# Last layer: four context slots left out of the projection, delta-rule preparation at two slots a tile

## What is computed

```python
for layer in range(DEPTH):
    need_ctx = layer < DEPTH - 1
    ...
def mixer(hc, hl, cos, sin, w_in, ..., need_ctx):
    pl = split_proj(hl @ w_in)
    pc = split_proj(hc @ w_in)
    r_l, r_c = retention_group(pc[0:4], pl[0:4], cos, sin, ret_rate, ret_norm_w, need_ctx)
    s_l, s_c = swa_group(pc[4:7], pl[4:7], cos, sin, sinks, need_ctx)
    g_l, g_c = gdn_group(pc[7:13], pl[7:13], conv_w, a_log, dt_bias, gdn_norm_w, need_ctx)
```

## Time and profile before

| | us |
|---|---|
| median of three runs | 3745.65 |
| their range | 3743.29 to 3751.66 |
| span of the profiled execution | 3739.8 |
| median less span | 5.85 |
| TensorE busy (of the span) | 3358.0 (90%) |
| VectorE busy | 1620.2 (43%) |
| ScalarE busy | 1050.0 (28%) |
| GpSimd busy | 670.9 (18%) |

### The profile page before, as it was taken

The page is one execution under the profiler, slowest core; times in us unless marked ns, Lnnn a source line. Parts: engine busy times, 40 slices in busy tenths (PEclk is TensorE's granted clock), DMA queues, the critical chain, the costliest instruction groups (busy, mean ns, idle before and its releaser), DMA issues. The chain is left out here.

```text
span 3739.8 us, 56640 instructions
## 1 busy us (share of the span) xinstructions
PE 3358.0 (90%) x21880; PEld 2813.4 (75%) x21880; DVE 1620.2 (43%) x2715; ACT 1050.0 (28%) x1921; POOL 670.9 (18%) x762
## 2 busy tenths in 40 slices
PE   6989847987899999999998989857887999999998
PEld 3878735866778888888887878746775778888886
DVE  4465775632352322223236365765633343322234
ACT  3244134612222121121213244134512231122112
POOL 1142763222000000000001142762222000000000
PEclk8999967998899999999999999967997999999998
DMA  4465285086401111111112466185194111111111
GB/s 175 145 195 189 71 276 159 18 240 199 162 28 39 40 38 35 39 39 39 34 39 83 147 192 198 62 279 150 27 274 172 57 45 51 45 50 46 50 50 62
DMA packets 245475, 396.49 MB, mean 106 GB/s; under 512 B 75811, under 2 KB 147747, under 8 KB 244902
## 3 DMA queue, kind: packets, MB, share of 16 engines
q1 hardware_dynamic: 239462, 374.03, 32.0%
q0 software_dynamic: 5824, 19.93, 1.4%
HBM read 280.27 MB, written 101.52 MB: 102 GB/s over the span
## 5 line engine op out<-in xcount | busy, mean ns | idle before, releaser
L1021 PE MATMUL ffn_bank<-ffn_h_hi,ffn_w_hi 128*128 128x512 f32 (+1 forms) x1760 | 651.4, 370 | 8.0 <-DVE ffn_h_lo L409 7.7
L1024 PE MATMUL ffn_bank<-ffn_h_lo,ffn_w_hi 128*128 128x512 f32 (+1 forms) x1760 | 649.1, 369 | 0.0
L1025 PE MATMUL ffn_bank<-ffn_h_hi,ffn_w_lo 128*128 128x512 f32 (+1 forms) x1760 | 648.6, 369 | 0.0
L924 PE MATMUL frt_acc<-frt_w_hi,frt_h_hi 128*128 128x472 f32 x960 | 377.3, 393 | 48.5 <-DVE frt_w_lo L803 27.6
L1021 PEld LDWEIGHTS ffn_bank<-ffn_h_hi,ffn_w_hi 128*128 128x128 f32 x1760 | 333.1, 189 | 72.3 <-DVE ffn_h_lo L409 13.2
L1025 PEld LDWEIGHTS ffn_bank<-ffn_h_hi,ffn_w_lo 128*128 128x128 f32 x1760 | 333.0, 189 | 55.3
L1024 PEld LDWEIGHTS ffn_bank<-ffn_h_lo,ffn_w_hi 128*128 128x128 f32 x1760 | 333.2, 189 | 54.2
L924 PE MATMUL frt_acc<-frt_w_hi,frt_h_lo 128*128 128x472 f32 x960 | 368.0, 383 | 0.0
L924 PE MATMUL frt_acc<-frt_w_lo,frt_h_hi 128*128 128x472 f32 x960 | 367.5, 383 | 0.0
L1015 DVE TENSOR_TENSOR ffn_w_lo<-ffn_raw,ffn_w_hi 128x1024 fp32r<-128x1024 f32 x132 | 161.7, 1225 | 469.2 <-ACT ffn_w_hi L1007 463.9
L1021 PE MATMUL ffn_bank<-ffn_a_hi,ffn_w_hi 128*128 128x512 f32 (+1 forms) x880 | 324.3, 368 | 0.8 <-DVE ffn_a_lo L1103 0.8
(11 more groups left out here) (370 smaller groups left out, 5597.5 us busy)
## 6 DMA issues: line engine op xcount, KB each, us to landing
ffn_raw<-w_ffn SPq DMA_DIRECT2D x132, 512.0 KB, 3.5
x<-ada_w SPq DMA_DIRECT2D x15, 2048.0 KB, 9.3
proj<-frt_out SPq DMA_DIRECT2D x120, 236.0 KB, 2.0
x<-proj SPq DMA_DIRECT2D x60, 384.0 KB, 4.5
frt_raw<-w_in SPq DMA_DIRECT2D x96, 236.0 KB, 4.4
met_pr<-proj SPq DMA_DIRECT2D x20, 704.0 KB, 6.1
met_vn<-pack SPq DMA_DIRECT2D x20, 640.0 KB, 6.7
pack<-frt_side SPq DMA_DIRECT2D x40, 256.0 KB, 2.5
```

Source lines behind the costliest of these rows:

```text
L924: mm = pe.matmul(acc[q % NA][:, 0:GW], a[:, k, tok], b[:, k, :], start=(k == 0 and i == 0), stop=(k == KC - 1 and i == 2))
L1021: mm = pe.matmul(out, w_hi, b_hi, start=first, stop=False)
L1024: pe.matmul(out, w_hi, b_lo, start=False, stop=False)
L1025: return pe.matmul(out, w_lo, b_hi, start=False, stop=last)
```

## The change

Attention values, keys and queries change places: values at 1552, keys at 1680, queries at 1808 to 2319; the gates stay. In the last layer the slots of tiles 0 and 1 are left out of groups whose first column is at or past `S_Q`, which is groups 4 (1888) and 5 (2360). Slots 0 to 39 are as before, group 4 is slots 40 to 47, group 5 slots 48 to 55. `base(j)` becomes `15 + 2 * j` in the last layer, so `SOLVE` is 39 there; `LATE` becomes 14. In both layers `meet` loads 1536 columns (the values lie between retention values and keys now, unused there), and the two adds of lines 1529 and 1530 become one of 640 columns.

```diff
-S_Q, S_K, S_V = 1552, 2064, 2192
+S_V, S_K, S_Q = 1552, 1680, 1808
-COLUMNS = ((2816, 16), (1792, 768), (0, 768), (1024, 768), (768, 256), (2560, 256))
+COLUMNS = ((2816, 16), (1792, 768), (0, 768), (1664, 128), (1536, 128), (1024, 512), (768, 256), (2560, 256))
...
-        SLOTS = GROUPS * TILES
+        WORK = [(g, t) for g in range(GROUPS) for t in range(TILES) if layer + 1 < DEPTH or t * P >= CTX or g * GW < S_Q]
+        SLOTS = len(WORK)
+        first_of = [min(q for q in range(SLOTS) if WORK[q][0] == g) for g in range(GROUPS)]
...
+        STEP = 12 if layer + 1 < DEPTH else 10
...
-            return 15 + (12 * j) // 5
+            return 15 + (STEP * j) // 5
...
-                for q in range(SOLVE):
-                    g, t = divmod(q, TILES)
+                for q in range(max(SOLVE, first_of[GROUPS - 2])):
+                    g, t = WORK[q]
...
-                LATE = 12
+                LATE = 2 * (first_of[GROUPS - 1] - SOLVE) - 4
...
-                    sp.dma_start(pr[u][:], proj[row:row + P, R_Q:R_Q + 1408]).then_inc(ins[u], 16)
+                    sp.dma_start(pr[u][:], proj[row:row + P, R_Q:R_Q + 1536]).then_inc(ins[u], 16)
...
-                    dve.tensor_tensor(hot[:, 0:512], hot[:, 0:512], swp[u][:, 0:512], ALU.add)
-                    dve.tensor_tensor(hot[:, 1024:1152], hot[:, 1024:1152], swp[u][:, 1024:1152], ALU.add)
-                    side = lambda ap: ap[:, 512:1024].rearrange("p (u c n) -> p u c n", u=2, c=4)
+                    dve.tensor_tensor(hot[:, 0:640], hot[:, 0:640], swp[u][:, 0:640], ALU.add)
+                    side = lambda ap: ap[:, 640:1152].rearrange("p (u c n) -> p u c n", u=2, c=4)
```

More of the change, by code:

```diff
@@ L632, in _ @@
                 for q in range(SLOTS):
-                    g, t = divmod(q, TILES)
-                    if t == 1 and g + 1 < GROUPS:
+                    g, t = WORK[q]
+                    if q == first_of[g] + 1 and g + 1 < GROUPS:
                         weights(g + 1)
@@ L679, in split_hi @@
                         else:
-                            act.wait_ge(psum_done, g * TILES)
+                            act.wait_ge(psum_done, first_of[g])
                         act.activation(w_hi[:, k, :], raw[:, k, :], ACT.Copy).then_inc(w_rounded, 1)
@@ L918, in project @@
                     for k in range(KC):
-                        if t == 0:
+                        if q == first_of[g]:
                             pe.wait_ge(w_split, g * KC + k + 1)
@@ L1281, in meet @@
         b_y, b_g, b_u = [st.ps(f"b_{n}", [P, 512]) for n in "ygu"]
-        pr, rp = [[st.sb(f"{n}{u}", shape) for u in range(NR)] for n, shape in (("pr", [P, 1408]), ("rp", [P, 2, 64]))]
+        pr, rp = [[st.sb(f"{n}{u}", shape) for u in range(NR)] for n, shape in (("pr", [P, 1536]), ("rp", [P, 2, 64]))]
         hot, swp = st.sb("hot", [P, 1152]), dual("swp", [P, 1152])
@@ L1303, in meet @@
         ident = mats[:, C_ID, :]
-        Q_R, V_R, Q_S = R_Q - R_Q, R_V - R_Q, S_Q - R_Q
+        Q_R, V_R, K_S = R_Q - R_Q, R_V - R_Q, S_K - R_Q
         with nc.Block() as block:
@@ L1391, in turn_second @@
                     spent(t, "skT")
-                    pe.transpose(b_k[:, 0:P], hot[:, 1024:1152], ident).then_inc(s["turned_k"], 1)
+                    pe.transpose(b_k[:, 0:P], hot[:, 512:640], ident).then_inc(s["turned_k"], 1)
                 turn_first(0)
@@ L1516, in rotate @@
                     dve.tensor_tensor(heads(hot[:, 0:512], 8), heads(pr[r][:, Q_R:Q_R + 512], 8), cos(8), ALU.mult)
-                    dve.tensor_tensor(heads(hot[:, 512:1152], 10), heads(pr[r][:, Q_S:Q_S + 640], 10), cos(10), ALU.mult).then_inc(s["rot"], 1)
+                    dve.tensor_tensor(heads(hot[:, 512:1152], 10), heads(pr[r][:, K_S:K_S + 640], 10), cos(10), ALU.mult).then_inc(s["rot"], 1)
                     if t == 0:
@@ L1592, in swap @@
                         pool.wait_ge(s["rotated"], t - 1)
-                    for base, hs, at in ((Q_R, 8, 0), (Q_S, 10, 512)):
+                    for base, hs, at in ((Q_R, 8, 0), (K_S, 10, 512)):
                         src = pr[r][:, base:base + hs * 64].rearrange("p (h a u f) -> p h a u f", h=hs, a=2, u=2)
```

## The result

| | before | after |
|---|---|---|
| median, us | 3746.53 (11 runs) | 3761.22 (11 runs) |
| range, us | 3736.02 to 3755.05 | 3750.21 to 3767.39 |
| span of the profiled execution, us | 3739.8 | 3762.3 |
| first copy of the last `front` to the start of the last `meet`, us | 368.9 | 391.4 |
| last `meet`, us | 123.0 | 117.4 |

The ratio of after to before is 1.004, with a 95% interval of 1.0026 to 1.0054. The forecast was 3732 us. The medians differ by 14.7 us and the two profiled executions by 22.5 us; single executions of either kernel scatter by more than 15 us, so the two agree.

What follows compares the result with a forecast made beforehand. TensorE was taken to bound the last layer's projection from slot 40, the solve hidden 5 us behind. Four slots' 20.5 us less slot 40's 6.7 us delay gave 13.8 us off 3745.65, so 3732 us; range 3723 to 3742 us.

Steps and rivals of the forecast that it cites:

- The four slots: Last layer's projection: four slots left out after slot 40, each 5.12 us and on the path, save 20.5 us.
- The round of the preparation: Last layer's loop of VectorE copy, SP stores, landing, products and convolution: 16.0 us, taken as 16.4 us a tile.
- Tile by tile: Last layer: tile 3's convolution 2 us earlier, tile 4's 4 us; tile 7's at 2246.2 us; slot 30 delayed 10.9 us.
- TensorE in the middle: Slots 16 to 39: TensorE waits only for split weights; longest wait, ahead of slot 30, grows from 8.0 to 12 us.
- From slot 40 to the end: Last projection stage: slot 40 copied 6.7 us later; slots 41 to 55 then take 80.4 us, ending 13.8 us earlier.
- The clock: TensorE's longer idle ahead of slot 30: nothing added; strict reading, half clock behind the gap, costs some 2 to 4 us.
- The solve: VectorE's solve starts near 2326 instead of 2336.3 us, ends at 2405.0 us, hidden 1.4 us before TensorE's end.
- `meet`: Both layers: wider loads cost at most 4.8 us, merged add saves up to 5 us; taken as cancelling, -4 to +5 us.
- A slower loop: Rival, 0.20: last layer's preparation takes 18.4 us a tile; gain only 3 to 8 us, total about 3740 us.
- The solve ends the stage late: Rival, 0.06: 20.8 us a tile throughout; solve ends at 2427 us, 6 us later than the stage before; about 3755 us.
- TensorE bounds all: Rival, 0.20: preparation loop runs at 14.7 us, slot 40 is not late, gain 20.5 us, total 3725 us.
- the change doesn't do what it says: Rival, 0.04: shorter group 4 makes TensorE wait for weights, or columns cost the attention stage something; 3745 us.

Runs made afterwards that it cites:

- e1: Changed kernel with the old tile spacing (STEP 12) restored in the last layer; four slots still left out, new columns kept: 3734.70 us, ratio 0.9978.
- e3: Changed kernel with all slots and the old spacing restored, keeping only the new column order and merged meet add: 3741.03 us, ratio 0.9986.
- e2: Changed kernel with all 60 slots restored in the last layer; two slots a tile and new columns kept: 3781.65 us, ratio 1.0101.
- e4: Changed kernel with GpSimd's two outer convolution taps cut to 8 of 768 columns in the last layer, a measurement only: 3739.82 us, ratio 0.9982.
- e5: Changed kernel with GpSimd doing the outer convolution taps one slot earlier in the last layer, nothing left out: 3741.81 us, ratio 0.999.
- e7: Changed kernel with the edits of e5 and e6 together in the last layer: 3730.23 us, ratio 0.9962.
- e9: e8 with the old spacing (STEP 12) in both layers, the changed kernel's slots still left out: 3714.89 us, ratio 0.9926.
- e6: Changed kernel with SP issuing phase 5's stores one slot earlier in the last layer, ahead of that slot's store: 3732.77 us, ratio 0.9966.
- e8: Changed kernel with the edits of e5 and e6 together in both layers: 3722.19 us, ratio 0.9942.
- e8b: e8 run once more, unchanged, beside e9 for comparison: 3721.77 us, ratio 0.9938.

## Why the prediction was wrong

**The four slots** were right: 20.5 us forecast, 20.5 between last copies in e1 and before, 22.0 between e1 and e3, 19.4 between e2 and the changed kernel.

**The round of the preparation** is the step that failed. Forecast: 5.0 + 1.4 + 2.5 + 1.6 + about 5.5 = 16.0 us, taken as 16.4. Measured: SP's issues 6.50 instead of 6.4, landing 2.50 instead of 2.5, products 1.80 instead of 1.6, the copy to the store 0.66, which the sum had not counted; and decay matrix to copy 9.34 instead of about 5.5. The structure was right; one term was short by 3.8 us. I had taken VectorE's instructions at the durations that they have alone (0.69, 0.69, 0.95, 0.96, 0.96 us) with a little on top. The rows to see it in were there: the earlier trace rows shows the same instruction at 0.95, 1.79 and 2.56 us. I never asked what stands beside it, and so never asked where GpSimd's work would lie once the store that frees GpSimd lands just behind the one that frees VectorE. In the loop it lies beside VectorE's each time; e4 prices the taps at 2.9 us a tile and e5 gets it back by moving them. The last microsecond of the 3.8 is what GpSimd's other products cost: they are still there in e4, where the part takes 6.34 us.

**The support from measured distances** misled. 16.4 and 16.9 us were distances of single pairs with a three-slot gap ahead of them, in which SP and VectorE had caught up. Where pair follows pair, I take it, that slack is not refilled. The bound of 20.8 us was in the text, as an exception with a reason of its own; it turned out to be the steady state.

**Tile by tile.** Tile 3 was to come 2 us earlier. It came 4.8 us later (2187.52 less the 2.4 us by which this stage began later, against 2180.25). Already tile 2's convolution lay beside GpSimd's taps and took 6.8 instead of 3.8 us, and its round, which holds the split of group 2's weights in both kernels, took 27.8 instead of 24.6 us. Tiles 3 to 7 then stood 20.8, 20.8, 21.5 and 21.8 us apart, and tile 7's convolution came 23.9 us later than the 2246.2 us forecast. The split of group 3's weights follows it by 8.8 us, as forecast:

```profile
2281.28 4.57 DVE L807 TENSOR_TENSOR frt_w_lo<-frt_raw,frt_w_hi 128x472 fp32r<-128x472 f32 x8 [2.06 <-ACT frt_w_hi L685]
```

So slot 30 was late by 34.7 us, where 10.9 was forecast. From there to the copy of slot 40 the forecast had 4.2 us less than before, since less preparation is left there; it took 5.0 us more, with 5 us of TensorE's waits for the preparation in it. Together these are the 39.8 us at slot 40: the rounds make 23.9 of the 33.1 us by which the forecast missed it, the stretch behind slot 30 the other 9.2.

**TensorE in the middle.** It was to wait 12 us for group 3's low weights and for nothing else. It waited 13.9 us in two waits for low weights, the longest 7.4, and 21.4 us for VectorE's and ScalarE's part of the preparation. That class of wait was missing in the sum. I read it as a result of the slow round: in e7 the waits for ScalarE's L737 (13.1 us) are gone, and 9.8 us of the others are left.

**From slot 40 to the end** 80.4 us were forecast and 83.7 measured. The slots are 5.12 us apart; the 3.2 us more lie at the last split, for which VectorE leaves the solve. Its wait for ScalarE was 11.01 us instead of 7.72, but that did not hold TensorE: TensorE waited 2.6 us in four waits there, exactly as before. What differs is the granted clock behind these waits. Six us of each kernel there, the changed one first, then the one before (columns as in the two stretches above):

```profile
2405.00:2411.00 6.00, 6.00 (x15) 4.68 (x16) 5.92 (x4) 0.56 (x1) 5.69 (x5) 0.50 0.11 40
2374.00:2380.00 6.00, 6.00 (x30) 5.28 (x29) 5.86 (x5) 1.13 (x2) 5.69 (x5) 1.00 0.12 43
```

TensorE is busy throughout in both, but at 1.2 instead of 2.4 GHz it does 15 matmuls instead of 30, and 15 matmuls at full clock are 3.2 us.

**The clock** was granted at 0.83 between 2160 and 2260 us, and there I find no time of its own that it cost, for the loop has no term of TensorE. Where TensorE bounds, at the last split, it cost the 3.2 us above. That is of the size, "some 2 to 4 us", that the prediction gave to a stricter reading for slot 30 and left out of its sum. The Trainium skill (page TensorE: Matmul & The Clock Gate, section Why this matters for your kernels) has it that gaps between bursts of matmuls bring the half clock back. The rows agree in the direction, but the gaps here are short: 1.94 us in the round, at most 0.8 us at the last split. Nor do such waits bring it back each time: of the twelve traces of this case, all with waits of at most 0.8 us and 1.2 to 2.7 us in total at the last split, seven show the half clock there (the changed kernel, e2, e3, e4, e5, e7, e9) and five do not (before, e1, e6, e8, e8b). What decides it is open, and so a few us of any difference between two profiled executions can come from it.

**The solve** was to start 10 us earlier and started 20.5 us later (2359.26 less 2.4, against 2336.32). It stayed hidden, by 6.2 us, where the forecast had 1.4.

**`meet`** was within its -4 to +5 us: -3.5 us in e3, -5.6 us in the changed kernel's last layer, +1.4 us in its first.

**The rivals.** "A slower loop" (0.20) named the right kind of failure, with 18.4 us a tile and a gain left over; the loop was slower still, and its reason, SP issuing without a break, explains only the terms that were near the forecast. "The solve ends the stage late" had the round, 20.8 us throughout, and the sign. Its mechanism was not what happened in the changed kernel, since slot 40 became so late that TensorE stayed behind the solve. The solve does end the stage in e1 and e9, but early, not late. The rival had been given 0.06 because 20.8 us was thought an exception. "TensorE bounds all" and "the change doesn't do what it says" are refuted by the waits of TensorE and by e1.

## What to carry to other kernels

Before a preparation is put closer together, write down its round as a closed loop through all queues, and give every instruction the duration that it has beside the work that is released on the other engines at the same time, not the one that it has alone. A distance seen once behind a pause may be a lower bound, and is no period. Where the loop runs over a queue of stores, moving a store ahead of the one that waits for the loop's last member can be worth more than a change of spacing: here one number in SP's program and one in GpSimd's, in both layers, were worth 19.8 us between the medians of e1 and e9, where slots and columns together had given 10.

## What the runs showed of the hardware

VectorE's product of two 128x768 fp32 tensors takes 0.95 us alone (e9) and 2.55 us beside GpSimd's product of the same size; GpSimd's takes 1.85 us alone (e5) and 2.25 to 2.55 us beside it. With 512 columns VectorE's takes 0.68 us alone and up to 1.53 us beside GpSimd. I had expected a share to be lost, not nearly two thirds of the speed. In the round shown above the two look as if they took turns: GpSimd's tap ends at 2210.06 and VectorE's product 0.8 us later, the next tap 1.7 us behind that at 2212.55, and VectorE's add (L857) again 0.8 us later. Each time that is a little less than the instruction takes alone, counted from the end of the other's. The Trainium skill (page SBUF — State Buffer, section Who interferes with whom) says that a VectorE instruction with two SBUF inputs contends with a GpSimd instruction that reads SBUF; these rows agree with it.
